# A transformer block kernel: order of the modulation groups' loads, and half of the first norm's shift as a bias

## The chip, the core and the metric
The program runs on one core of one Trainium2 chip. The metric is the device time of one execution in microseconds (us); lower is better. TensorE (PE) multiplies, VectorE (DVE), ScalarE (ACT) and GpSimd (POOL) work on elements, SyncE (SP) issues the loads. PSUM has eight banks of 128 x 512 float32; matmul outputs land there.

## What is computed
One layer over 256 latent and 256 context tokens of width 2048, all in float32. What matters here is its beginning:

```
mods  = silu(c) @ w_mod + b_mod            # 2048 x 12288, for c and for c_ctx
n     = rmsnorm(h) * gain * (1 + scale) + shift      # the first norm: amul = gain * (1 + scale)
proj  = n @ w_in                           # columns: 512 q, 256 kv, 64 rotary, then 3 x 1024 for a short convolution
q_a   = rmsnorm(q), kv_a = rmsnorm(kv), the rotary part is rotated
```

Context tokens need the kv and rotary columns alone. Attention, the convolution's gating, an output projection, routing to 4 of 32 experts and the experts' products follow.

## The kernel before, in words
The rows of the model's width lie on the 128 partitions: 16 row blocks k, four of them a set s. nT holds the transposed, normed tokens, columns 0 to 255 latent, 256 to 511 context. w_mod is worked in groups of 512 columns. Group g = s holds the shift of set s, group g = 4 + s its scale. For the first eight groups in load order (n = 0 to 7) TensorE makes the row products: 16 blocks k, each a pair of instructions, four blocks at once in four column quarters of the array (`first_rows` L706, `group_rows` L695, all in bank 7). ScalarE copies the 128 x 512 result to `part` (`rows_out` L1254), TensorE transposes it back into bank 7 (`mod_cols_of` L663), VectorE reduces it into modT (`cols_out` L1565). Only then may the next group use bank 7 (`step_group` L775 waits for modT_done). Before, `MOD_ORDER` (L345) is shift 0, scale 0, shift 1, scale 1 and so on; when both of a set are there, VectorE adds the biases, forms amul, and scales and shifts the set's four latent blocks of nT (L1618 to L1633); ScalarE does so for the context (L1271 to L1278).

The input products of a set are `query_set` (16 matmuls of 256 columns, L750), `kv_set` (4 of 512 columns, twice, L767) and `rotary_set` (4 of 512 columns on half of the array's columns, L760), which accumulate over the four sets in banks 0 to 6. TensorE's order is written out by hand (L780 to L811): the products of set s stand between the rows of the groups of set s+1. Set 3 comes last, then the squares' sums (`ones` matmuls into banks 7 and 4), with the rotary matmuls (L804, L805) in between. Then come four turns of the convolution's columns (L823 to L834), each of six blocks of 16 matmuls of 256 columns (`conv_blocks` L814).

From group 8 on the row products are VectorE's: 16 steps over 128 x 512 for each group (`accumulate` L1572), two groups a turn, begun in turn 0 only after VectorE has finished the norms of q and kv (L1646 to L1665). TensorE sums them over the partitions with `mod_sum_cols` (L677), which waits for the 16 steps: group 8 between the second and the third pair of blocks of turn 0 (L830), group 9 after the third (L834).

SyncE issues all loads on one queue, in the order of its program: x, constants, ctx, group 0, group 1, the input columns of set 0 (`load_in(0)`), then groups 2 and 3 and `load_in(1)`, and so on (L393 to L438). Groups 2 to 7 use seven buffers in turn (`load_early` L407), each load waiting until TensorE used the buffer. `load_conv` (L441) and `load_group` (L420) follow; group 9's four loads wait for VectorE's steps of group 8 (`freed_by_dve` L430), and turn 1's first convolution load is issued behind them (L451 to L453).

Of the kernel before, what the change touches and what calls it, by code (L numbers as in the profile page):

```python
# [9 lines left out]
ACT = mybir.ActivationFunctionType  # L10
# [5 lines left out]
P = 128  # L16
# [94 lines left out]
def block_kernel(nc, x, c, ctx_in, c_ctx, w_mod, b_mod, attn_norm, w_in, q_a_norm, w_q_b, kv_a_norm, w_kv_b,  # L111
                 conv_w, o_norm_mla, o_norm_conv, w_out, ffn_norm, w_router, router_bias,
                 w_exp_gate, w_exp_up, w_exp_down, w_sh_gate, w_sh_up, w_sh_down, final_norm, consts, out):
    with ExitStack() as stack:
# [71 lines left out]
        WI_SEM = (2, 0, 1, 5)  # L186
# [4 lines left out]
        EARLY_USES = [4, 4, 4, 3, 3, 4, 4] + [0] * 5  # L191
        rowq, rowkv = kq[:, 0:T], kq[:, T:3 * T]
# [45 lines left out]
        def yparts_of(t):  # L238
# [13 lines left out]

        BANKS_C, BANKS_H, BANKS_B = (1, 0), (2, 3), (4, 0)
# [18 lines left out]
        ctxs_ready = sem("ctxs_ready")  # L272
        xT_lat, xT_ctx = sem("xT_lat"), sem("xT_ctx")
# [6 lines left out]
        stat_q, stat_kv, q_ready, kv_ready = (sem("stat_q"), sem("stat_kv"),  # L280
                                                        sem("q_ready"), sem("kv_ready"))
# [14 lines left out]
        rt_rows, rt_copied, rt_full, rt_sig, mask_ready, rank_full, rank_ready = (  # L296
            sem("rt_rows"), sem("rt_copied"), sem("rt_full"), sem("rt_sig"), sem("mask_ready"), sem("rank_full"),
# [7 lines left out]
        sort_in, tbl_full, tbl_out, sort_full, cols_in = (sem("sort_in"), sem("tbl_full"), sem("tbl_out"),  # L305
                                                          sem("sort_full"), sem("cols_in"))
# [62 lines left out]
        def _(sp):  # L369
# [63 lines left out]
            for s in range(1, 4):  # L433
                for n in (2 * s, 2 * s + 1):
                    load_early(n)
                if s == 1:
                    sp.wait_ge(mod_rows, 1)
                load_in(s)  # L438
# [8 lines left out]
            sp.wait_ge(q_full, 1)  # L447
# [164 lines left out]
        def _(pool):  # L612
            nc.gpsimd.memset(csT[:, :, :], 0.0).then_inc(zeroed, 1)
            nc.gpsimd.memset(upad[:, :, :], 0.0).then_inc(zeroed, 1)

# [36 lines left out]
        def _(pe):  # L652
# [67 lines left out]
            def rows_T(rows, done, side):  # L720

                for j in range(KC // 2):
                    if j >= 3:
                        pe.wait_ge(done, j - 2)
                    for k in (2 * j, 2 * j + 1):
                        for t in range(2):
                            at = T * (k % 2) + 128 * t
                            ins = nc.tensor.transpose(ps[:, 2 * (j % 3) + side, at:at + 128], rows[:, t, 128 * k:128 * k + 128],
                                                      ident)
                    ins.then_inc(xT_full, 1)  # L730

            pe.wait_ge(xs_ready, 2)
            rows_T(xs, xT_lat, 0)
            pe.wait_ge(small_done, 1)
            for k in range(8):
                first_rows(0, k)
            pe.wait_ge(ctxs_ready, 2)
            rows_T(ctxs, xT_ctx, 1)
            for k in range(8, KC):
                first_rows(0, k)  # L740
            mod_cols_of(FIRST, 0, 7)
            pe.wait_ge(modT_done, 1)
            for k in range(KC):
# [35 lines left out]

            for s in range(SETS - 1):  # L780
                query_set(s, range(4) if s == 0 else (0, 1))
                if s == 0:
                    kv_set(s, 0)
                step_group(2 * s + 2)
                if s:
                    kv_set(s, 0)
                mod_cols_of(2 * s + 2, 0, 7)
                rotary_set(s)
                if s:
                    query_set(s, (2, 3))  # L790
                step_group(2 * s + 3)
                mod_cols_of(2 * s + 3, 1, 7)
                kv_set(s, 1)
            query_set(SETS - 1, range(4))
            kv_set(SETS - 1, 0)
            rotary_set(SETS - 1)
            pe.wait_ge(modT_done, 8)
            pe.wait_ge(q_sq, 4)
            for m in range(4):
                ins = mm(ps[:, 7, 0:T], ones, squ[:, T * m:T * m + T], m == 0, m == 3)  # L800
            ins.then_inc(stat_q, 1)
            pe.wait_ge(q_out, 4)
            pe.wait_ge(kr_sum, 1)
            mm(ps[:, 2, :], cst[:, C_DUP:C_DUP + P], krs[:, :], True, True)  # L804
            mm(ps[:, 3, 0:T], cst[:, C_ROTK:C_ROTK + P], krs[:, 0:T], True, True).then_inc(kr_mm, 1)  # L805
            kv_set(SETS - 1, 1)
            pe.wait_ge(kv_out, 1)
            pe.wait_ge(kv_sq, 2)
            for m in range(2):
                ins = mm(ps[:, 4, :], ones, squ[:, 1024 + 512 * m:1536 + 512 * m], m == 0, m == 1)  # L810
            ins.then_inc(stat_kv, 1)  # L811


# [9 lines left out]
            with pe.Fori(0, 4) as i:  # L823
# [11 lines left out]
            pe.wait_ge(y_out, 8)  # L835

# [162 lines left out]
            ins.then_inc(rt_rows, 1)  # L999
# [42 lines left out]
            nc.tensor.transpose(ps[:, 6, 0:128], vrow[:, :], ident).then_inc(tbl_full, 1)  # L1042
            shared_up(0, 1, range(8, 10))
            pe.wait_ge(tbl_out, 1)
# [190 lines left out]
        def _(sc):  # L1235
# [27 lines left out]

            for j in range(KC // 2):
                sc.wait_ge(xT_full, KC // 2 + j + 1)
                copy(nT[:, 2 * j:2 * j + 2, T:2 * T], ps[:, 2 * (j % 3) + 1, :].rearrange("p (k t) -> p k t", k=2))\
                    .then_inc(xT_ctx, 1)
            rows_out(0, 7, 0, True)
            rows_out(1, 7, 1, True)
            sc.wait_ge(xT_ctx, KC // 2)  # L1270
            for s in range(SETS):  # L1271
                if s:
                    rows_out(2 * s, 7, 0, False)
                    rows_out(2 * s + 1, 7, 1, False)
                sc.wait_ge(amul_ready, s + 1)
                for k in range(4 * s, 4 * s + 4):
                    nc.scalar.activation(nT[:, k, T:2 * T], nT[:, k, T:2 * T], ACT.Identity, bias=modT[:, k, 1:2],
                                         scale=amul[:, k, 1:2]).then_inc(nT_ctx, 1)  # L1278


            for m in range(4):
                sc.wait_ge(q_full, m + 1)
                nc.scalar.activation(squ[:, T * m:T * m + T], ps[:, m, 0:T], ACT.Square).then_inc(q_sq, 1)
            sc.wait_ge(kr_full, 1)
            copy(krs[:, :], ps[:, 6, :]).then_inc(kr_sum, 1)

            def kv_square(m):
                sc.wait_ge(kv_full, m + 1)
                nc.scalar.activation(squ[:, 1024 + 512 * m:1536 + 512 * m], ps[:, 4 + m, :], ACT.Square).then_inc(kv_sq, 1)
# [118 lines left out]
            sc.wait_ge(rt_rows, 1)  # L1408
            copy(part[:, 0, 0:T], ps[:, 4, 0:T]).then_inc(rt_copied, 1)
            sc.wait_ge(rt_full, 1)  # L1410
# [110 lines left out]
        def _(ve):  # L1521
# [35 lines left out]
            ve.wait_ge(zeroed, 2)  # L1557
# [50 lines left out]
            for j in range(KC // 2):  # L1608
                ve.wait_ge(xT_full, j + 1)
                V.tensor_copy(nT[:, 2 * j:2 * j + 2, 0:T], ps[:, 2 * (j % 3), :].rearrange("p (k t) -> p k t", k=2))\  # L1610
# [4 lines left out]
            cols_out(0, MOD_ORDER[0], 7)  # L1615
            cols_out(1, MOD_ORDER[1], 7)
            ve.wait_ge(xT_lat, KC // 2)
            for s in range(SETS):  # L1618
                if s:
                    for n in (2 * s, 2 * s + 1):  # L1620
                        cols_out(n, MOD_ORDER[n], 7)
                ve.wait_ge(modT_done, 2 * s + 2)
                for at in (4 * s, 4 * (s + 4)):
                    ins = V.tensor_tensor(modT[:, at:at + 4, :], modT[:, at:at + 4, :],
                                          bT[:, at:at + 4].unsqueeze(2).to_broadcast([P, 4, 2]), ALU.add)
                link(ins)
                V.scalar_tensor_tensor(out=amul[:, 4 * s:4 * s + 4, :], in0=modT[:, 16 + 4 * s:20 + 4 * s, :], scalar=1.0,
                                       in1=vecT[:, V_AN + 4 * s:V_AN + 4 * s + 4].unsqueeze(2).to_broadcast([P, 4, 2]),
                                       op0=ALU.add, op1=ALU.mult).then_inc(amul_ready, 1)
                ve.wait_ge(amul_ready, s + 1)  # L1630
                for k in range(4 * s, 4 * s + 4):
                    V.tensor_scalar(nT[:, k, 0:T], nT[:, k, 0:T], amul[:, k, 0:1], modT[:, k, 0:1], ALU.mult, ALU.add)\
                        .then_inc(nT_lat, 1)  # L1633


            for m in range(4):
                ve.wait_ge(q_sq, m + 1)
                V.tensor_scalar(qaT[:, m, :], ps[:, m, 0:T], vecT[:, V_QN + m:V_QN + m + 1], None, ALU.mult)\
                    .then_inc(q_out, 1)

            def kv_gain(m):
                ve.wait_ge(kv_sq, m + 1)
                V.tensor_scalar(kvT[:, m, :], ps[:, 4 + m, :], vecT[:, V_KN + m:V_KN + m + 1], None, ALU.mult)\
                    .then_inc(kv_out, 1)

            kv_gain(0)  # L1646
            ve.wait_ge(stat_q, 1)
# [491 lines left out]
```

## Time and profile before

| | us |
|---|---|
| median of 3 runs (1107.96 to 1110.99) | 1109.44 |
| span of the profiled execution, first to last instruction | 1107.5 |
| TensorE busy | 1011.4 (91%) |
| VectorE busy | 549.5 (50%) |
| ScalarE busy | 221.2 (20%) |
| loaded, mean rate | 380.3 MB, 343 GB/s |

The profiled execution has no time of its own in the list of runs; its span lies 1.9 us below their median, which holds the same work and what lies around it. A timeline row is: start, duration, engine, line, operation, output<-inputs, count, and in brackets the engine's idle time before it with what ended it. Every float32 matmul is two instructions, so x32 stands for 16 matmuls. Durations of neighbours overlap a little; distances of starts tell what a piece costs. L654 is the helper that all matmuls share.

### The profile page before, as it was taken

To read this page: it belongs to the slowest core of one execution; us is meant where nothing else is said; L and a number is where in the kernel's file an instruction comes from. 1 tells how busy PE (TensorE), PEld (TensorE's weight loads), DVE (VectorE), ACT (ScalarE), POOL (GpSimd) and SP (SyncE) were. 2 spreads that over 40 slices of the span, in tenths; PEclk is the share of its full clock that TensorE was granted. 3 is DMA by queue.
4 is the path that set the end of the run, shared out by engine and by line. 5 is a ranking of instruction groups with operands and counts; after the bars stand their busy time and mean duration, and the time that the engine had idled before them with its cause. 6 is when DMAs were issued, how large, how long until landed. Compare 5 with 4: busy or idle time off the path is not lost.

```text
span 1107.5 us, 15664 instructions
## 1 busy us (share of the span) xinstructions
PE 1011.4 (91%) x6004; PEld 566.6 (51%) x6005; DVE 549.5 (50%) x1082; ACT 221.2 (20%) x442; POOL 20.3 (2%) x28
## 2 busy tenths in 40 slices
PE   3889999999999889999998999998899898998985
PEld 2534578888885345444485645433334333344421
DVE  3000186854824694985582234545246344545524
ACT  5211110000002363010341213222113112213212
POOL 0000000000002001000000000000000000000002
PEclk9899999999999999999999999999999998999998
DMA  9999979999854747999739999999999999999994
GB/s 358 389 389 389 377 232 359 372 345 328 284 181 169 256 144 262 387 387 335 230 130 367 371 405 403 406 408 407 409 409 406 408 407 408 409 407 408 409 406 180
DMA packets 158359, 380.30 MB, mean 343 GB/s; under 512 B 10498, under 2 KB 44112, under 8 KB 157136
## 3 DMA queue, kind: packets, MB, share of 16 engines
q1 hardware_dynamic: 158288, 379.35, 91.3%
q8 instruction: 45, 0.74, 0.3%
q14 instruction: 26, 0.21, 0.1%
HBM read 377.22 MB, written 2.10 MB: 342 GB/s over the span
## 4 chain that ended last, share of the span: by engine, by line
PE 64%; DMA 13%; SPq 12%; DVE 6%; issue 2%; ACT 2%; POOL 0%; ACTq 0%; DVEq 0%; POOLq 0%
PE ps L654 64%; DMA ring<-in_w_exp_down 7%; SPq L537 4%; SPq L532 4%; DVE part L1590 3%; DMA ring<-in_w_exp_up 2%; DMA ring<-in_w_in 1%; DMA ring<-in_w_mod 1%; DMA qnT<-in_w_mod 1%; SPq L397 1%; DVE tiny L1736 1%; SPq L417 1%; DVE xres L2021 1%; SPq L394 1%; SPq L395 0%
## 5 line engine op out<-in xcount | busy, mean ns | idle before, releaser
L654 PE MATMUL ps<-nreg,ring 128*128 128x256 f32 (+2 forms) x1312 | 306.9, 398 | 6.7 <-DVE ring L1741 4.1
L654 PEld LDWEIGHTS ps<-nreg,ring 128*128 128x128 f32 (+1 forms) x1312 | 243.8, 190 | 63.1 <-issue 30.8
L1590 DVE SCALAR_TENSOR_TENSOR part<-ring,csT,part 128x512 f32<-128x512 f32 x232 | 174.7, 753 | 8.6
L654 PE MATMUL ps<-ring,nreg 128*32 128x512 f32 (+1 forms) x1344 | 174.2, 602 | 3.6 <-DMA ring<-in_w_exp_up 3.2
L654 PE MATMUL ps<-ring,conv 128*32 128x512 f32 (+2 forms) x688 | 104.5, 663 | 23.0 <-DMA ring<-in_w_exp_down 22.1
L654 PE MATMUL ps<-ring 128*128 128x512 f32 x256 | 110.7, 592 | 0.0
L654 PEld LDWEIGHTS ps<-ring,nreg 128*32 128x32 f32 (+1 forms) x1344 | 49.1, 115 | 111.7 <-issue 111.6
L2021 DVE TENSOR_TENSOR xres<-xres,ps 128x512 f32<-128x512 f32 x96 | 61.6, 683 | 48.9 <-PE ps L654 48.9
L654 PEld LDWEIGHTS ps<-ring 128*128 128x128 f32 x256 | 48.6, 190 | 60.4 <-issue 60.0
L654 PEld LDWEIGHTS ps<-ring,conv 128*32 128x32 f32 (+2 forms) x688 | 30.2, 125 | 88.4 <-issue 83.9
L654 PE MATMUL ps<-pick,qnT 128*128 128x128 bf16 x384 | 67.8, 221 | 2.8 <-DMA ring<-in_w_exp_up 2.8
L654 PE MATMUL ps<-nreg,conv 128*128 128x512 bf16 x228 | 57.9, 379 | 11.0 <-DVE xres L2021 8.7
L654 PE MATMUL ps<-pick,kq 128*128 128x128 bf16 x384 | 67.7, 221 | 0.0
L654 PE MATMUL ps<-pick,hb 128*128 128x128 bf16 x384 | 67.6, 220 | 0.0
L1977 DVE TENSOR_SCALAR nreg<-ps,amul,modT 128x128 f32<-128x128 f32 x96 | 32.8, 404 | 45.6 <-PE ps L654 45.6
L654 PEld LDWEIGHTS ps<-pick,qnT 128*128 128x128 bf16 x384 | 37.8, 98 | 24.4 <-issue 23.1
L2005 DVE TENSOR_TENSOR nreg<-ps,qkv 128x512 f32<-128x512 f32 x44 | 30.2, 687 | 34.6 <-PE ps L654 34.4
L1568 DVE TENSOR_REDUCE modT<-ps 128x8 f32<-128x32 f32 x8 | 1.5, 192 | 88.0 <-PE ps L669 88.0
L1996 DVE SCALAR_TENSOR_TENSOR conv<-ps,tiny,conv 128x256 f32<-128x256 f32 x12 | 5.8, 484 | 74.0 <-ACT conv L1445 74.0
L654 PEld LDWEIGHTS ps<-nreg,conv 128*128 128x128 bf16 x228 | 19.9, 97 | 41.1 <-issue 24.0
L1237 ACT ACTIVATE conv<-ps 128x256 f32<-128x256 f32 x20 | 7.7, 383 | 160.2 <-PE ps L654 139.5
L1435 ACT ACTIVATE nreg<-ps,modT,amul 128x128 f32<-128x128 f32 x96 | 35.9, 457 | 14.6 <-PE ps L654 14.6
(265 smaller groups left out, 883.9 us busy)
## 6 DMA issues: line engine op xcount, KB each, us to landing
ring<-in_w_mod SPq DMA_DIRECT2D x78, 1024.0 KB, 10.9
ring<-in_w_exp_gate SPq DMA_DIRECT2D x128, 512.0 KB, 13.6
ring<-in_w_exp_up SPq DMA_DIRECT2D x128, 512.0 KB, 15.1
ring<-in_w_exp_down SPq DMA_DIRECT2D x128, 512.0 KB, 14.4
ring<-in_w_in SPq DMA_DIRECT2D x12, 2048.0 KB, 13.4
ring<-in_w_out SPq DMA_DIRECT2D x8, 2048.0 KB, 11.6
ring<-in_w_mod SPq DMA_DIRECT2D x3, 2048.0 KB, 19.7
ring<-in_w_in SPq DMA_DIRECT2D x3, 1664.0 KB, 15.7
```

What stands on the lines that cost most here:

```text
L394: sp.dma_start(k_of(s, 8), mod_block(MOD_ORDER[0], 8 * s, 8)).then_inc(w_full[s], 16)
L397: sp.dma_start(early[q + 3], mod_block(MOD_ORDER[1], 4 * q, 4)).then_inc(unit_in[q + 3], 16)
L417: sp.dma_start(early[j % 7], mod_block(MOD_ORDER[n], 4 * q, 4)).then_inc(unit_in[j % 7], 16)
L532: sp.dma_start(unit(n)[:, 1024 * g:1024 * g + 1024], src[:, bass.ds(e, 1), q, :].rearrange("p a x -> p (a x)")).then_inc(unit_in[PLACE[n]] ...
L537: sp.dma_start(unit(n)[:, 1024 * k:1024 * k + 1024], wd[:, bass.ds(e, 1), k, 1024 * h:1024 * h + 1024].rearrange("p a x -> p (a x)"))\
L654: return nc.tensor.matmul(o, l, r, start=start, stop=stop)
L1435: ins = nc.scalar.activation(xg[:, k, :], ps[:, b % 2, 128 * j:128 * j + 128], ACT.Identity, bias=modT[:, 3 * KC + k, 0:1], scale=amul2[:, ...
L1590: ins = V.scalar_tensor_tensor(out=out_, in0=w_, scalar=scale, in1=acc_, op0=ALU.mult, op1=ALU.add)
L1736: link(V.tensor_reduce(rowmax[:, b:b + 2], ps[:, SCORE_BANK[b]:SCORE_BANK[b] + 2, :], AX.X, ALU.max))
L1977: ins = V.tensor_scalar(xg[:, k, :], ps[:, b % 2, 128 * j:128 * j + 128], amul2[:, k:k + 1], modT[:, 3 * KC + k, 0:1], ALU.mult, ALU.add)
L2005: V.tensor_tensor(ylast[n] if last else ygate[:, n % 2, :], ps[:, 4 + n % 2, :], gfB[:, 512 * n:512 * n + 512], ALU.mult)\
L2021: V.tensor_tensor(xres[:, h, cols], xres[:, h, cols], ps[:, 6 + h, :], ALU.add)\
```

## The change
- `MOD_ORDER` becomes [4, 5, 6, 2, 7, 3, 0, 1]: scales of sets 0, 1, 2, shift 2, scale 3, shift 3, and last the shifts of sets 0 and 1. `load_in(s)` comes earlier in the queue, and `WI_SEM` swaps two buffers.
- For sets 0 and 1 (`LATE = 2`) nT is only scaled. The input products of these sets are made without their shift.
- When shifts 0 and 1 are there, VectorE writes them into `shift_cols`, and TensorE multiplies them with the input columns of the eight blocks (`shift_products`, 8 matmuls of 512 and 8 of 320 columns, four at once), ScalarE copies the rows, and seven small matmuls turn them into columns (`bias_columns`). They enter as a bias: in ScalarE's squares and rotary copy, in VectorE's gain products.
- The eight latent blocks get their shift added afterwards (8 more VectorE instructions of 256 columns), for the convolution's products; their first block of turn 0 is split in two (`first_conv`).
- The first turn of the convolution loop is peeled. The squares' sums of q and kv and the rotary matmuls (`in_squares`) move behind the first two blocks of turn 0. ScalarE copies q raw first and squares it later; three operations over 512 columns become two of 256 each.
- Semaphores are joined (stat_q and stat_kv, rt_rows and rt_full, tbl_full and sort_full), TensorE's wait for kr_done moves behind the loop, and GpSimd has two more memsets (128 x 256 and 128 x 14).

```diff
-        MOD_ORDER = [g for s in range(4) for g in (s, s + 4)]
+        MOD_ORDER = [4, 5, 6, 2, 7, 3, 0, 1]
+        LATE = 2
...
+            load_in(0)
             sp.dma_start(k_of(5, 8), mod_block(MOD_ORDER[1], 0, 8)).then_inc(w_full[5], 16)
             for q in (2, 3):
                 sp.dma_start(early[q + 3], mod_block(MOD_ORDER[1], 4 * q, 4)).then_inc(unit_in[q + 3], 16)
-            load_in(0)
...
+            sp.wait_ge(mod_rows, 1)
+            load_in(1)
+            load_early(2)
+            load_in(2)
+            load_early(3)
+            load_early(4)
+            load_in(3)
+            for n in (5, 6, 7):
+                load_early(n)
...
             load_group(8, 12, mslot, freed_by_pe)
-            sp.wait_ge(q_full, 1)
+            sp.wait_ge(shift_full, 2)
             load_conv(0, 1, CONV0 + 2 * CW)
...
+            for s in range(1, SETS):
+                query_set(s, range(4))
+                step_group(2 * s)
+                kv_set(s, 0)
+                mod_cols_of(2 * s, 0, 7)
+                step_group(2 * s + 1)
+                rotary_set(s)
+                mod_cols_of(2 * s + 1, 1, 7)
                 kv_set(s, 1)
...
+            def shift_products():
+                pe.wait_ge(shift_ready, LATE)
+                pe.wait_ge(q_sq, 4)
+                for bank, at, end in ((2, 0, QL), (3, QL, WI)):
+                    for k in range(4 * LATE):
+                        ins = mm(ps[32 * (k % 4):32 * (k % 4) + 32, bank, 0:end - at], shift_cols[:, k, :],
+                                 wiq[k // 4][:, k % 4, at:end], k < 4, k >= 4 * LATE - 4)
+                    ins.then_inc(shift_full, 1)
+            def bias_columns():
+                pe.wait_ge(shift_out, 2)
+                for m in range(6):
+                    mm(ps[:, 7, 384 + 2 * m:386 + 2 * m], shift_rows[:, 128 * m:128 * m + 128], sum4[:, 0:2], True, True)
+                mm(ps[0:64, 7, 396:398], shift_rows[:, KR0:WI], sum4[:, 0:2], True, True).then_inc(shift_full, 1)
...
+            first_conv(range(4 * LATE, KC))
+            shift_products()
+            first_conv(range(4 * LATE))
+            bias_columns()
+            conv_blocks(0, 0, BANKS_C, (1,))
+            in_squares()
+            conv_blocks(0, 1, BANKS_H)
+            pe.wait_ge(kv_out, 2)
+            mod_sum_cols(8, 0)
+            pe.wait_ge(gc_out, 2)
+            pe.wait_ge(mean_wide, 2)
+            conv_blocks(0, 2, BANKS_B)
+            mod_sum_cols(9, 1)
+            with pe.Fori(1, 4) as i:
...
             kv_gain(0)
-            ve.wait_ge(stat_q, 1)
+            ve.wait_ge(stat_full, 1)
+            ve.wait_ge(kr_mm, 1)
+            ve.wait_ge(q_out, 4)
             mean_square_wide(rowq, ps[:, 7, 0:T], QL)
```

## Rows read from the trace of the kernel before

**Rows 1.** Busy time by stretch; columns: PE, PEld, DVE, ACT, POOL, clock, DMA share, GB/s

```profile
80.10:105.93 25.83, 24.48 (x128) 12.02 (x129) 2.18 (x9) 3.27 (x6) 0.00 (x0) 1.00 1.05 389
105.93:121.36 15.43, 14.71 (x80) 6.96 (x81) 0.19 (x1) 1.19 (x2) 0.00 (x0) 1.00 1.05 385
```

**Rows 2.** Chain that ended last, whole span, in order of time

```profile
65.84 14.22 DMA ring<-in_w_mod
...
91.81 14.07 DMA qnT<-in_w_mod
...
144.59 226.50 PE ps L654 x1038
```

**Rows 3.** Timeline of PE, 36 to 121 us

```profile
36.10 1.92 PE L654 MATMUL ps<-ring,csT 128*32 128x512 f32 x16 [0.28 <-DVE modT L1568]
...
80.10 1.07 PE L654 MATMUL ps<-ring,csT 128*32 128x512 f32 x8 [1.64 <-DMA ring<-in_w_mod]
81.10 3.70 PE L654 MATMUL ps<-nreg,ring 128*128 128x512 f32 x8
84.64 0.60 PE L669 MATMUL ps<-cst,part 128*128 128x128 f32 x4
85.17 5.59 PE L654 MATMUL ps<-nreg,ring 128*64 128x512 f32 x24
90.68 1.06 PE L654 MATMUL ps<-qnT,csT 128*32 128x512 f32 x8
...
116.51 1.07 PE L654 MATMUL ps<-hb,csT 128*32 128x512 f32 x8
...
118.25 1.90 PE L654 MATMUL ps<-ring,csT 128*32 128x512 f32 x16
```

**Rows 4.** Timeline of PE, 137 to 175 us

```profile
137.10 1.99 PE L654 MATMUL ps<-kq,cst 128*128 128x256 f32 x8
138.93 1.45 PE L654 MATMUL ps<-krs,cst 128*128 128x512 f32 x4
140.22 3.60 PE L654 MATMUL ps<-nreg,ring 128*128 128x512 f32 x8
144.59 1.95 PE L654 MATMUL ps<-kq,cst 128*128 128x512 f32 x4 [0.78 <-ACT kq L1289]
146.39 27.79 PE L654 MATMUL ps<-nreg,ring 128*128 128x256 f32 x128
174.01 0.95 PE L654 MATMUL ps<-cst,qnT 128*128 128x1 f32 x8
```

**Rows 5.** Timeline of DVE, 140 to 166 us

```profile
140.42 0.42 DVE L1650 COPY krT<-ps 128x256 f32<-128x256 f32 x1 [0.86 <-PE ps L654]
...
142.01 1.75 DVE L1540 RECIPROCAL kq<-kq 128x256 f32<-128x256 f32 x1
144.56 0.75 DVE L1643 TENSOR_SCALAR qkv<-ps,vecT 128x512 f32<-128x512 f32 x1 [0.80 <-ACT kq L1289]
...
146.59 0.69 DVE L1535 TENSOR_SCALAR kq<-ps 128x512 f32<-128x512 f32 x1
147.97 3.35 DVE L1540 RECIPROCAL kq<-kq 128x512 f32<-128x512 f32 x1 [0.69 <-ACT kq L1296]
...
152.57 0.48 DVE L1583 TENSOR_SCALAR part<-ring,csT 128x512 f32<-128x512 f32 x1
...
164.11 1.12 DVE L1590 SCALAR_TENSOR_TENSOR qnT<-ring,csT,part 128x512 f32<-128x512 f32 x1
```

**Rows 6.** Timeline of ACT, 126 to 140 us

```profile
126.72 0.38 ACT L1283 ACTIVATE kq<-ps 128x256 f32<-128x256 f32 x1 [2.38 <-PE ps L654]
...
139.61 0.42 ACT L1296 ACTIVATE kq<-kq 128x256 f32<-128x256 f32 x1
```

**Rows 7.** Busy time by stretch, around the wait before 43.58 us; columns as in rows 1

```profile
39.90:43.50 3.60, 0.66 (x4) 0.42 (x4) 1.99 (x8) 2.01 (x5) 0.00 (x0) 1.00 1.03 389
...
44.90:48.30 3.40, 3.40 (x10) 2.69 (x9) 0.00 (x0) 0.00 (x0) 0.00 (x0) 0.53 1.05 386
```

**Rows 8.** Timeline of PE at 43.58 us

```profile
43.58 12.26 PE L654 MATMUL ps<-nreg,ring 128*128 128x256 f32 x40 [2.46 <-DMA ring<-in_w_in]
55.77 1.06 PE L654 MATMUL ps<-qkv,csT 128*32 128x512 f32 x8
```

**Rows 9.** Timeline of SP, load of turn 1's first convolution block

```profile
166.00 0.39 SPq L442 DMA_DIRECT2D ring<-in_w_in  x1
```

More of the change, by code:

```diff
@@ L718, in first_rows, with rows_T @@
                     ins.then_inc(mod_rows, 1)
-            def rows_T(rows, done, side):
-                for j in range(KC // 2):
+            def rows_T(rows, done, banks, js):
+                for j in js:
                     if j >= 3:
@@ L778, in step_group @@
                 group_rows(n, 7)
[L780 to L787, printed above, removed]
+            query_set(0, (0, 2))
+            pe.wait_ge(xT_ctx, KC // 2)
+            query_set(0, (1, 3))
+            pe.wait_ge(modT_done, 1)
+            for k in range(KC):
+                first_rows(1, k)
@@ new lines, in bias_columns, with in_squares @@
+            def bias_columns():
[3 more added lines that the diff above has]
+                mm(ps[0:64, 7, 396:398], shift_rows[:, KR0:WI], sum4[:, 0:2], True, True).then_inc(shift_full, 1)
+            def in_squares():
+                pe.wait_ge(q_sq, 8)
+                for m in range(4):
+                    ins = mm(ps[:, 7, 0:T], ones, q_squ[:, T * m:T * m + T], m == 0, m == 3)
+                ins.then_inc(stat_full, 1)
+                pe.wait_ge(kr_sum, 1)
+                mm(ps[:, 6, :], cst[:, C_DUP:C_DUP + P], krs[:, :], True, True)
+                mm(ps[:, 7, T:2 * T], cst[:, C_ROTK:C_ROTK + P], krs[:, 0:T], True, True).then_inc(kr_mm, 1)
+                pe.wait_ge(kv_out, 1)
+                pe.wait_ge(kv_sq, 2)
+                for m in range(2):
+                    ins = mm(ps[:, 4, :], ones, squ[:, 1024 + 512 * m:1536 + 512 * m], m == 0, m == 1)
+                ins.then_inc(stat_full, 1)
@@ L814, in conv_blocks, with first_conv @@
+            def first_conv(ks):
+                w = k_of(0, KC)
+                for n, k in enumerate(ks):
+                    if k < 4 * LATE:
+                        pe.wait_ge(nT_shift, k + 1)
+                    ins = mm(ps[:, BANKS_C[0], 0:T], w[:, k, 0:128], nT[:, k, 0:T], k == 4 * LATE, k == 4 * LATE - 1)
+                if ks[-1] == 4 * LATE - 1:
+                    ins.then_inc(conv_full, 1)
             def conv_blocks(i, s, banks, ms=(0, 1)):
@@ L1281, in _ @@
             for m in range(4):
                 sc.wait_ge(q_full, m + 1)
-                nc.scalar.activation(squ[:, T * m:T * m + T], ps[:, m, 0:T], ACT.Square).then_inc(q_sq, 1)
+                copy(q_raw[:, m, :], ps[:, m, 0:T]).then_inc(q_sq, 1)
+            for n in (6, 7):
+                rows_out(n, 7, n % 2, False)
+            for n in range(2):
+                sc.wait_ge(shift_full, n + 1)
+                at, end, bank = ((0, QL, 2), (QL, WI, 3))[n]
+                copy(shift_rows[:, at:end], ps[:, bank, 0:end - at]).then_inc(shift_out, 1)
@@ L1284, in _ @@
+            sc.wait_ge(shift_ready, LATE + 1)
+            for m in range(4):
+                sc.wait_ge(q_sq, m + 1)
+                nc.scalar.activation(q_squ[:, T * m:T * m + T], q_raw[:, m, :], ACT.Square, bias=in_bias[:, m, 0:1])\
+                    .then_inc(q_sq, 1)
             sc.wait_ge(kr_full, 1)
-            copy(krs[:, :], ps[:, 6, :]).then_inc(kr_sum, 1)
+            for v in range(2):
+                ins = nc.scalar.activation(krs[:, T * v:T * v + T], ps[:, 6, T * v:T * v + T], ACT.Identity,
+                                           bias=in_bias[:, 6, v:v + 1])
@@ L1287, in kv_square @@
+            ins.then_inc(kr_sum, 1)
             def kv_square(m):
                 sc.wait_ge(kv_full, m + 1)
-                nc.scalar.activation(squ[:, 1024 + 512 * m:1536 + 512 * m], ps[:, 4 + m, :], ACT.Square).then_inc(kv_sq, 1)
+                for v in range(2):
+                    ins = nc.scalar.activation(squ[:, 1024 + 512 * m + T * v:1280 + 512 * m + T * v],
+                                               ps[:, 4 + m, T * v:T * v + T], ACT.Square, bias=in_bias[:, 4 + m, v:v + 1])
+                ins.then_inc(kv_sq, 1)
@@ L1614, in _, with scale_of @@
             V.tensor_scalar(ctxs[:, 0, :], ctxs[:, 0, :], tiny[:, 10:11], None, ALU.mult).then_inc(ctxs_ready, 1)
[L1615 to L1616 removed]
             ve.wait_ge(xT_lat, KC // 2)
[L1618 to L1629 removed]
+            def scale_of(n):
+                cols_out(n, MOD_ORDER[n], 7)
+                ve.wait_ge(modT_done, n + 1)
+                at = 4 * MOD_ORDER[n]
+                link(V.tensor_tensor(modT[:, at:at + 4, :], modT[:, at:at + 4, :],
+                                     bT[:, at:at + 4].unsqueeze(2).to_broadcast([P, 4, 2]), ALU.add))
+                return V.scalar_tensor_tensor(out=amul[:, at - 16:at - 12, :], in0=modT[:, at:at + 4, :], scalar=1.0,
+                                              in1=vecT[:, V_AN + at - 16:V_AN + at - 12].unsqueeze(2).to_broadcast([P, 4, 2]),
+                                              op0=ALU.add, op1=ALU.mult)
@@ new lines, in shift_of @@
+            def shift_of(n, out_):
+                cols_out(n, MOD_ORDER[n], 7)
+                ve.wait_ge(modT_done, n + 1)
+                at = 4 * MOD_ORDER[n]
+                return V.tensor_tensor(out_, modT[:, at:at + 4, :], bT[:, at:at + 4].unsqueeze(2).to_broadcast([P, 4, 2]), ALU.add)
+            for s in range(SETS):
+                n = (0, 1, 2, 4)[s]
+                if s < LATE:
+                    scale_of(n).then_inc(amul_ready, 1)
+                else:
+                    link(scale_of(n))
+                    shift_of(n + 1, modT[:, 4 * s:4 * s + 4, :]).then_inc(amul_ready, 1)
@@ new lines, in _ @@
+                    ins.then_inc(nT_lat, 1)
+            for s in range(LATE):
+                shift_of(6 + s, shift_cols[:, 4 * s:4 * s + 4, 0:2]).then_inc(shift_ready, 1)
+                ve.wait_ge(shift_ready, s + 1)
+                ve.wait_ge(mod_rows, 2 * s + 3)
+                for k in range(4 * s, 4 * s + 4):
+                    V.tensor_scalar(nT[:, k, 0:T], nT[:, k, 0:T], shift_cols[:, k, 0:1], None, ALU.add).then_inc(nT_shift, 1)
+            ve.wait_ge(shift_full, 3)
+            V.tensor_copy(tiny[:, 16:28], ps[:, 7, 384:396])
```

139 lines of the change are left out of this document (62 added, 77 removed).

## The prediction

> **What bounds the kernel now.** I read the chain that ended last first, then busy times by stretch, then the timelines of TensorE and VectorE where the change lies. Up to 106 us the chain runs through transfers: TensorE resumes at 80.10 and at 105.93 when a group's last quarter has landed [rows 2, 3], and the core loads at 389 and 385 GB/s throughout [rows 1]. But TensorE is nearly full there too: of 25.83 us it works 24.48 [rows 1]. From 144.59 on the chain is 226.5 us of matmuls without a gap [rows 2]. So two things count: when TensorE enters the convolution turns, and whether it then still runs without a gap.
>
> The second has one neighbour that is close. VectorE starts group 8's 16 steps at 152.57, and the last ends at 164.11 + 1.12 = 165.23 [rows 5]; TensorE asks for them at 174.01 [rows 4]. That is 8.8 us of slack, and the whole change must be read against it.
>
> **Prices.** Distances of starts: a kv half set 84.64 − 81.10 = 3.54; the transposes of a group 85.17 − 84.64 = 0.53; half a query set with a rotary set 90.68 − 85.17 = 5.51; a group's rows 116.51 to 118.25 + 1.90 = 3.6 [rows 3]. 128 instructions over 256 columns take 27.6 us [rows 4], 0.216 each: 6.9 for a query set or a convolution block (32), 3.45 for 16, so the rotary set is 2.05. The q sum is 138.93 − 137.10 = 1.85, the rotary matmuls 1.3, the kv sum 146.39 − 144.59 = 1.8 [rows 4].
>
> **When the loads allow it.** Between the landings at 80.06 and 105.89 lie two groups and one set of input columns, 9856 KB: 2.68 us per 1024 KB. In the new order group 5's last quarter stands where group 6's stood, less one group (4096 KB, −10.7) and plus one set of input columns (1664 KB, +4.4): it lands at 99.5, is used by 100.5. Set by set TensorE needs 6.9 + 2 x 3.6 + 2 x 3.54 + 2.05 + 2 x 0.53 = 24.3 us, the loads 25.8, so TensorE waits there for this landing, and what happened before it (the earlier start of the products, the transposes' new place) is absorbed. Groups 6 and 7 land by 121, about when asked for. Their buffers are freed by TensorE's rows; the last of them is asked for some 7 us ahead of its use, tight, but behind others still in the queue. The first convolution load follows by 127. I cost all these moves at nothing; the cover is the queue, and without it a load of 1024 KB costs at least 2.7 us.
>
> **From 100.5 to the rotary matmuls' end.** Rotary sets 2 x 2.05 = 4.1; transposes 3 x 0.53 = 1.6; kv half sets 3 x 3.54 = 10.6; query set 3 6.9; rows of groups 6 and 7 7.2; two convolution blocks 13.8; q sum 1.85 and rotary 1.3. New: step_group stands right behind the transposes in the same bank, so it waits for VectorE's reduction, 0.4 (0.28 idle in the row of that kind [rows 3]).
>
> Shift products: 8 matmuls over 832 columns in all. A group's rows, 16 over 512 columns in the same four quarters, take 3.6 us [rows 3], so these take 3.6 x (8 x 832) / (16 x 512) = 2.9. Were the quarters to go one after another, the nearest price is 3.54 for four full matmuls: 11.5 us. I take 2.9, from the same shape.
>
> The Trainium skill, TensorE: Matmul & The Clock Gate, Measured speedup vs the span model, gives three column tiles 2.38 times the speed of one, not 3. By that ratio an estimate for four is 3.5 us and the total 0.6 later. The row of this very shape decides, and it shows nearly the full factor.
>
> Bias columns: seven matmuls with full weights and two moving columns. The row with eight instructions of one column lasts 0.95, about 0.1 each [rows 4]; 14 make 1.4, nothing at the least and 3.0 at most, at the 0.216 of an instruction with 256 columns. The same skill page, Wait — 56ns, not 53.3ns?, says that matmuls start no closer than about 25 ns apart however few columns they have; an estimate from that is 0.35, and the total 1.1 earlier. The row shows four times as much for this shape, so the sum keeps the row.
>
> Together 4.1 + 1.6 + 10.6 + 6.9 + 7.2 + 13.8 + 3.15 + 0.4 + 2.9 + 1.4 = 52.1: the rotary matmuls end at 152.6. The other work has cover: ScalarE's raw copies and squares at 0.38 each [rows 6] lie under 6.9 us of convolution block; the eight VectorE additions under the last kv half set and the convolution's first half; GpSimd's memsets under the first load.
>
> **TensorE's own finish.** in_squares now waits for kv_square(1), which stands on ScalarE behind the root of q, which waits for VectorE after the rotary matmuls: mean square 0.43, root 0.42 [rows 6], two squares 0.76 and hand-overs 0.2 make 1.8 idle. Then the kv sum 1.8 and two blocks 13.8: TensorE asks for group 8 at 170.0, 4.0 earlier than 174.01. That is all the reordering gains, after the 4.3 us of new matmuls and the two new waits (0.4 and 1.8) are paid.
>
> **VectorE's tail, the step that decides.** From 152.6, in VectorE's order: mean square 0.45 (a pass over 256 columns, as the root's 0.42 [rows 6]); rotation 142.01 − 140.42 = 1.6; reciprocal 1.75; kv gain in two halves 0.8; four q products 1.4 (inside 146.59 − 144.56 [rows 5]): it reaches kv's mean square at 158.6. Before, that stood at 146.59, so this piece is 12.0 later: the sums were moved behind two convolution blocks, and nothing of VectorE's was moved ahead of them. From there to the end of group 8's steps it was 165.23 − 146.59 = 18.6 [rows 5], with 3.35 of reciprocal in it, and no part of that is touched. So group 8 is ready at 177.3. TensorE stands idle 7.3 us, and goes on 177.3 − 174.0 = **3.3 us later** than before. Group 9 is ready at 189.9, asked for after 191: no second wait. Turn 1's first load, issued behind group 8's last step (before at 166.00 [rows 9]), is out at 178, landed by 188, needed at 193.
>
> **The clock.** After a stretch of 3.6 us with only 0.66 of work the granted clock was 0.53 of full (1.2 GHz) from 44.90 to 48.30 [rows 7]. 48 instructions then took 55.77 − 43.58 = 12.2 [rows 8] where 6.9 + 3.54 = 10.45 would do: 1.75 lost. A wait of 7.3 us is longer, so I add 1.75; bounds are 0 (the wait of 1.64 before 80.10 [rows 3] lost nothing) and twice that.
>
> **Sum.** +3.3 + 1.75 = +5.05 on a stretch after which every later stage hangs on TensorE's progress. Profile 1107.5 + 5.0 = 1112.5; the median stands 1.9 above the span, so 1109.44 + 5.05 = 1114.5.
>
> **Rivals.**
> - VectorE's tail is the wait, the clock keeps up or falls briefly: +3.3, 1112.7. For it: after the wait before 43.58 the clock fell only at 44.90, with TensorE at work again [rows 7, 8], so the fall does not follow a wait at once and here may lie inside it. Chance 0.22, on both sides of the bound.
> - TensorE stays the bound. If VectorE's way from the rotary matmuls to group 8's end took under 17.4 us, the 4.0 would stay: 1105.4, **faster**. It decides at exactly that point; the rows sum it to 24.7, and nothing in the diff starts the accumulation earlier. For it only that my reading of VectorE's order could be wrong. Chance 0.12.
> - Front and tail cancel: the chain up to 152.6 is 1.5 to 3 us shorter than my distances say, or the clock falls within the wait and is back early: +0.5 to +2.5, 1111. Chance 0.14.
> - A late load: a bubble in the queue at group 7's last quarter, or a low clock in the waits near 98, or slower shift products (towards 11.5): each delays both engines alike, +7 to +9, 1117.5. Chance 0.10.
> - The change does not do what it says: then no shift group loads last, both traces agree, 1109.4; inside the third case.
> - Forecast: 0.42.
>
> **Numbers.** The range takes the forecast, the second and fourth case and most of the third: 1109.0 to 1118.5; left out is mostly the faster case. A measurement of this kernel tells 0.3% (3.3 us) from no change. Slower by more: 0.42 + 0.11 + 0.10 = 0.63. Within: 0.11 + 0.14 = 0.25. Faster: 0.12.
>
> **What would show it.** Right: TensorE idle 6 to 8 us at about 170 before mod_sum_cols of group 8, released by VectorE; the rotary matmuls ending near 152.6; VectorE's first step of group 8 near 164.6; clock at half after it. Wrong: that wait under 2 us, or TensorE's chain reaching the end of turn 0's second pair before 168 or after 172, or the landing of group 5 off 99.5.

## The result, and the profile after

| | before | after |
|---|---|---|
| median, us | 1109.50 (4 runs, 1107.96 to 1110.99) | 1115.14 (4 runs, 1114.78 to 1116.25) |
| ratio to before, 95% interval | | 1.005 [1.0036, 1.0064] |
| span of the profiled execution | 1107.5 | 1114.4 |
| TensorE busy | 1011.4 | 1013.5 |
| VectorE busy | 549.5 | 551.6 |

The change costs 5.6 us (1115.14 − 1109.50); 1114.5 was forecast. The two totals of busy time do not tell where: the changed kernel's trace lacks 22 of TensorE's records behind 414 us (4239 where the kernel before has 4261), and work at half clock counts as busy. The chain tells.

The chain that ended last, changed kernel (start, duration, what). It answers to [rows 2]:

```profile
87.82 10.90 DMA ring<-in_w_mod
...
98.76 2.93 PE ps L666 x16
...
153.51 15.77 PE ps L666 x68
169.28 7.16 issue
176.44 83.59 PE ps L666 x390
```

Ahead of the convolution turns the last wait for a transfer is at 98.7. New is a gap of 7.16 us at 169.28, in a stretch where the chain before had none. It is booked as "issue", the name for time with no releaser that the profile can name. The timeline of TensorE around it, changed kernel, answers to [rows 3, 4]:

```profile
98.76 1.06 PE L666 MATMUL ps<-ring,csT 128*32 128x512 f32 x8 [1.30 <-DMA ring<-in_w_mod]
99.76 1.94 PE L666 MATMUL ps<-nreg,ring 128*64 128x512 f32 x8
...
120.55 1.06 PE L666 MATMUL ps<-hb,csT 128*32 128x512 f32 x8 [0.28 <-DVE modT L1637]
...
133.46 3.00 PE L666 MATMUL ps<-ring,yspare 128*32 128x512 f32 x32
136.39 3.72 PE L666 MATMUL ps<-nreg,ring 128*128 128x256 f32 x16
139.95 1.60 PE L666 MATMUL ps<-cst,hb 128*128 128x2 f32 x14
141.48 7.17 PE L666 MATMUL ps<-nreg,ring 128*128 128x256 f32 x32
148.49 1.89 PE L666 MATMUL ps<-hb,cst 128*128 128x256 f32 x8
150.22 1.45 PE L666 MATMUL ps<-krs,cst 128*128 128x512 f32 x4
153.51 1.96 PE L666 MATMUL ps<-kq,cst 128*128 128x512 f32 x4 [1.84 <-ACT kq L1356]
155.31 13.98 PE L666 MATMUL ps<-nreg,ring 128*128 128x256 f32 x64
176.44 1.84 PE L666 MATMUL ps<-cst,qnT 128*128 128x1 f32 x8 [7.16 <-issue]
178.14 15.75 PE L666 MATMUL ps<-nreg,ring 128*128 128x256 f32 x64
193.73 0.95 PE L666 MATMUL ps<-cst,qnT 128*128 128x1 f32 x8
194.54 27.87 PE L666 MATMUL ps<-nreg,ring 128*128 128x256 f32 x128
```

The row at 176.44 is group 8's sum. TensorE was ready for it at 169.28, 4.7 us earlier than before (174.01), and got it 2.4 us later. The releaser is found on VectorE, timeline of the changed kernel, answering to [rows 5]:

```profile
151.77 0.42 DVE L1604 TENSOR_SCALAR kq<-ps 128x256 f32<-128x256 f32 x1 [5.74 <-issue]
...
157.72 0.69 DVE L1604 TENSOR_SCALAR kq<-ps 128x512 f32<-128x512 f32 x1
159.10 3.35 DVE L1609 RECIPROCAL kq<-kq 128x512 f32<-128x512 f32 x1 [0.70 <-ACT kq L1365]
...
163.70 0.48 DVE L1652 TENSOR_SCALAR part<-ring,csT 128x512 f32<-128x512 f32 x1
...
175.24 1.09 DVE L1659 SCALAR_TENSOR_TENSOR qnT<-ring,csT,part 128x512 f32<-128x512 f32 x1
...
192.54 0.16 DVE L1666 COPY modT<-ps 128x4 f32 x1 [0.27 <-DVE conv L1783]
```

Group 8's last step ends at 175.24 + 1.09 = 176.33, and TensorE starts 0.1 us later. VectorE works from 151.77 on with one break, 0.70 us for ScalarE's root at 159.10, but it sat idle for 5.74 us before that. Its first step of group 8 went from 152.57 to 163.70.

Busy time by stretch, changed kernel (columns as in rows 1; the one behind POOL is the granted clock):

```profile
171.80:176.40 4.60, 0.00 (x0) 0.00 (x0) 4.42 (x7) 0.00 (x0) 0.00 (x0) 0.50 0.99 347
176.44:181.90 5.46, 5.46 (x18) 4.77 (x19) 5.21 (x8) 0.00 (x0) 0.00 (x0) 0.53 0.96 328
182.00:185.40 3.40, 3.40 (x18) 2.99 (x17) 3.22 (x6) 0.00 (x0) 0.00 (x0) 1.00 1.10 348
```

The clock fell some 2 us into the wait (0.92 granted from 169.30 to 171.70, 0.50 behind that), and TensorE came back at half clock (1.2 GHz) and kept it for about 5.1 us: from 181.50 on the granted clock is 0.99. From 176.44 to 193.73 it took 17.29 us for what took 188.72 − 174.01 = 14.71 before, so 2.6 us were lost. Turn 1 starts 5.01 us later than before (194.54 against 189.53).

Nothing is won back or lost up to the first scores, and then the profiled execution loses once more. Timeline of TensorE, kernel before:

```profile
371.96 1.95 PE L654 MATMUL ps<-ring,qnT 128*128 128x512 f32 x4 [0.88 <-DVE ring L1723]
...
394.60 1.96 PE L654 MATMUL ps<-nreg,ring 128*128 128x256 f32 x8 [2.17 <-DVE ring L1741]
```

and changed kernel:

```profile
376.97 1.96 PE L666 MATMUL ps<-ring,qnT 128*128 128x512 f32 x4 [0.88 <-DVE ring L1820]
...
399.61 3.35 PE L666 MATMUL ps<-nreg,ring 128*128 128x256 f32 x8 [2.18 <-DVE ring L1838]
```

Both stretches lie 5.01 us apart, with the same wait of 2.2 us before the second row; but the same eight instructions took 3.35 instead of 1.96 us. The granted clock from 400.5 to 403.9 was 0.57 in this execution. With the matmuls behind them that is 1.7 us more (from the second row to TensorE's next wait for VectorE 14.36 instead of 12.66), and with the 5.01 it makes up all but 0.2 of the 6.9 us between the two spans. The other three executions of the changed kernel had spans of 1113.0 to 1113.4, so part of it is this execution's own.

### The profile page after: what moved, and what is told of

The parts are those of the page before. It is cut to its first block, busy times and chain, and to the rows that moved or that the text cites. A ratio compares the mean times of both kernels' runs of the same rounds, so it can differ in the third digit from the quotient of the medians.

```text
span 1114.4 us, 15752 instructions
## 1 busy us (share of the span) xinstructions
PE 1013.5 (91%) x6028; PEld 569.5 (51%) x6051; DVE 551.6 (50%) x1094; ACT 223.3 (20%) x451; POOL 20.6 (2%) x30
## 4 chain that ended last, share of the span: by engine, by line
PE 60%; SPq 15%; DMA 13%; DVE 6%; issue 4%; ACT 2%; POOL 0%; ACTq 0%; DVEq 0%; POOLq 0%
PE ps L666 59%; SPq L542 8%; DMA ring<-in_w_exp_down 7%; SPq L547 6%; DMA ring<-in_w_mod 3%; DVE part L1659 3%; DMA ring<-in_w_exp_up 2%; DMA qkv<-in_w_mod 1%; DVE tiny L1833 1%; SPq L553 1%; DVE xres L2118 1%; PE ps L740 0%; ACT nreg L1472 0%; DVE nreg L1609 0%; ACT ring L1465 0%
## 5 line engine op out<-in xcount | busy, mean ns | idle before, releaser
L666 PE MATMUL ps<-ring,conv 128*32 128x512 f32 (+2 forms) x688 | 102.1, 647 | 25.4 <-DMA ring<-in_w_exp_down 24.6
L666 PE MATMUL ps<-nreg,conv 128*128 128x512 bf16 x207 | 53.3, 379 | 13.3 <-DVE xres L2118 8.7
## 6 DMA issues: line engine op xcount, KB each, us to landing
ring<-in_w_mod SPq DMA_DIRECT2D x78, 1024.0 KB, 11.2
```

The source lines that it names most:

```text
L666: return nc.tensor.matmul(o, l, r, start=start, stop=stop)
```

## The experiments

All nine are measured against the kernel before, run on the same chip (three series; its medians there were 1110.01, 1109.33 and 1109.29). Two numbers are read from each: the total, and when TensorE starts turn 1's blocks. The second comes from one profiled execution. Totals of two runs whose intervals overlap are not told apart.

| run | ratio to before, 95% interval | wait before group 8's sum | turn 1 starts, us |
|---|---|---|---|
| kernel before | | 0 | 189.53 |
| the change | 1.0050 [1.0036, 1.0064] | 7.16 | 194.54 |
| half of group 8 early | 0.9993 [0.9981, 1.0005] | 0 | 187.82 |
| all of group 8 early | 0.9957 [0.9944, 0.9970] | 0 | 185.08 |
| wait filled | 1.0039 [1.0025, 1.0054] | 0.30 | 193.98 |
| sums moved, nothing else | 1.0105 [1.0090, 1.0120] | 8.12 | 200.63 |
| sums ahead of the second block | 1.0013 [1.0001, 1.0024] | 0.26 | 188.99 |
| all early, kv square first | 0.9949 [0.9932, 0.9965] | 0 | 182.77 |
| kv square first, alone | 1.0062 [1.0047, 1.0077] | 9.23 | 195.53 |
| group 8 asked for later | 1.0075 [1.0059, 1.0092] | moved, 8.95 | 194.79 |
| before, quarter of group 8 early | 1.0001 [0.9989, 1.0012] | 0 | 189.53 |

### Half of group 8's steps early

```diff
             kv_gain(0)
+            accumulate(8, 0, quarters=range(2), by_feature=True)
             ve.wait_ge(stat_full, 1)
...
-            with ve.Fori(0, 4) as i:
+            def turn(i, group8):
...
+            turn(0, range(2, 4))
+            with ve.Fori(1, 4) as i:
+                turn(i, range(4))
```

> Changed kernel, but VectorE does 8 of group 8's 16 steps (about 5.8 us) in its idle time between the first kv gain and the wait for the q sum. Theory (VectorE's tail before group 8 is what TensorE waits for, and the wait costs the clock too): the wait of 7.16 us before group 8's sum falls to 1 to 2 us, no low clock follows it, the third pair of convolution blocks of turn 0 starts near 171.5 instead of 178.1, and the time is about 7.5 us under the changed kernel's, near 1107.5. Rival (the 4.3 us of added matmuls and late loads are what costs, the wait is only where TensorE gets ahead of them): the time stays within 2 us of 1115, and another wait appears later, for a load or for group 9.

Median 1108.88 us beside 1110.01 for the kernel before. Timeline of TensorE in this run:

```profile
153.96 3.04 PE L666 MATMUL ps<-kq,cst 128*128 128x512 f32 x4 [1.98 <-ACT kq L1356]
...
171.26 0.95 PE L666 MATMUL ps<-cst,qnT 128*128 128x1 f32 x8
...
186.93 1.02 PE L666 MATMUL ps<-cst,qnT 128*128 128x1 f32 x8 [0.81 <-DVE modT L1666]
```

The wait before group 8's sum is gone, and with it the loss, although every added matmul is still there: 5.6 us hung on VectorE being late. The forecast of 1107.5 was 1.4 too low. Two details were not expected. The clock fell at 154.9 here, after the wait for the kv square (0.53 up to 158.3), so TensorE was 1.7 us slower up to 171.26 and met a group 8 that was just ready. And group 9's sum now waits 0.81 us for modT: the sum of group 9 may use its bank only after VectorE took group 8's out of it, and that copy stands behind group 9's 16 steps and the convolution's taps. I had checked only the 16 steps.

### All of group 8's steps early

```diff
+            accumulate(8, 0, by_feature=True)
             ve.wait_ge(shift_full, 3)
             V.tensor_copy(tiny[:, 16:28], ps[:, 7, 384:396])
...
+            turn(0, ())
+            with ve.Fori(1, 4) as i:
+                turn(i, range(4))
```

> Changed kernel, but all 16 steps of group 8 stand in VectorE's idle time of 13.3 us before it waits for the bias columns. Theory: no wait before group 8's sum at all; TensorE starts the third pair near 170.1, 4.7 us ahead of the kernel before, if the loads of group 8 (issued from 123.4 on) land by 140; time near 1105, some 4.5 us under the kernel before. Should the fourth quarter land late, the bias copy is late by as much and the squares' sums of q take it over beyond 2.4 us. Rival (added matmuls and loads): no better than the kernel before.

Median 1104.88 us, 5.1 under the 1110.01 of the kernel before. The timeline of VectorE shows the 16 steps in the idle time that the change opened, with the loads nearly in time:

```profile
129.30 0.49 DVE L1652 TENSOR_SCALAR part<-ring,csT 128x512 f32<-128x512 f32 x1 [0.61 <-DMA ring<-in_w_mod]
129.82 11.19 DVE L1659 SCALAR_TENSOR_TENSOR part<-ring,csT,part 128x512 f32<-128x512 f32 x14
...
142.03 0.17 DVE L1728 COPY tiny<-ps 128x12 f32<-128x12 f32 x1
```

The bias copy is at 142.03 instead of 141.59, inside its cover. TensorE's timeline has no wait before the third pair:

```profile
170.38 14.06 PE L666 MATMUL ps<-nreg,ring 128*128 128x256 f32 x64
```

It starts where 170.1 was expected, and 4.4 us ahead of the kernel before. So the change as a whole does gain something on TensorE, added matmuls paid; as made it gives that away to VectorE's order. How much of the gain is the loads' order alone, no run separates; the run with the move alone, below, shows that the move brings only 0.6 us of it (TensorE asks for group 8 at 181.51 − 8.12 = 173.39 instead of 174.01).

### The wait filled with matmuls

```diff
+            pe.wait_ge(kr_done, 1)
+            for _ in range(8):
+                mm(ps[:, 6, :], ident, cst[:, 0:512], True, True)
             pe.wait_ge(kv_out, 2)
             mod_sum_cols(8, 0)
```

> Changed kernel with 8 float32 matmuls over 512 columns into a free bank (6.9 us at full clock) put into TensorE's wait before group 8's sum. They compute nothing that is used. Theory: TensorE still goes on when group 8 is ready, at 176.4, but at full clock: the sum's 8 instructions take 0.95 instead of 1.84 us and the 64 behind them 13.9 instead of 15.6; time 2.6 us under the changed kernel's, near 1112.5. If the low clock came from something else, the time stays at 1115; if the matmuls ran past the wait, it would rise.

Median 1114.12 beside 1110.01, 4.1 more, where the change alone had 5.6 and 2.6 less was expected. The intervals of the two ratios overlap, so a gain is not shown. Timeline of TensorE:

```profile
169.25 7.03 PE L666 MATMUL ps<-cst 128*128 128x512 f32 x16
176.58 1.02 PE L666 MATMUL ps<-cst,qnT 128*128 128x1 f32 x8 [0.30 <-issue]
177.47 14.06 PE L666 MATMUL ps<-nreg,ring 128*128 128x256 f32 x64
192.97 1.14 PE L666 MATMUL ps<-cst,qnT 128*128 128x1 f32 x8 [1.45 <-DVE modT L1669]
193.98 29.43 PE L666 MATMUL ps<-nreg,ring 128*128 128x256 f32 x128
...
377.97 1.95 PE L666 MATMUL ps<-ring,qnT 128*128 128x512 f32 x4 [0.88 <-DVE ring L1823]
```

The clock part is shown for its stretch: at full clock the same 64 instructions take 13.9 instead of 15.6 us. But TensorE then only arrives earlier at the next thing that VectorE owes it, waits 1.45 us, and the clock falls there (0.50 from 193.8 to 197.0; the 128 instructions take 29.43 instead of 27.87). In the changed kernel that second wait is missing because the low clock had used it up: VectorE's copy is at 192.54, TensorE asks at 193.73. So of the clock's 2.6 us hardly any was to be had: turn 1 starts only 0.56 us earlier than in the changed kernel (193.98 against 194.54), and the fall behind it takes that back, with the first scores at 377.97 against 376.97. My expectation had left out the second wait.

### The move alone, on the kernel before

```diff
-            kv_set(SETS - 1, 0)
-            rotary_set(SETS - 1)
-            pe.wait_ge(modT_done, 8)
-            pe.wait_ge(q_sq, 4)
...
+            kv_set(SETS - 1, 0)
+            rotary_set(SETS - 1)
+            kv_set(SETS - 1, 1)
+            pe.wait_ge(modT_done, 8)
+            pe.wait_ge(q_out, 4)
...
+            conv_blocks(0, 0, BANKS_C)
+            in_squares()
+            pe.wait_ge(kr_done, 1)
+            conv_blocks(0, 1, BANKS_H)
```

> Kernel before, with one thing of the change: the squares' sums of q and kv and the rotary matmuls stand behind the first two convolution blocks of turn 0 instead of ahead of them. Order of loads and shift stay as they were. Theory: VectorE reaches group 8 some 16 us later (mean square of q at 156.4, q and kv done and 16 steps at 181.7), TensorE asks at 173.7 and waits 8 us, then runs 2 us at low clock: +9.5 us, near 1119. Rival (the loss comes from the new order of loads or from the added matmuls): within 2 us of the kernel before.

The q sum, the rotary matmuls and the kv sum are unchanged and stand in in_squares. Median 1121.22 beside 1110.01: +11.2 us, where +9.5 was expected. Timeline of TensorE:

```profile
181.51 1.83 PE L654 MATMUL ps<-cst,qnT 128*128 128x1 f32 x8 [8.12 <-issue]
183.20 16.78 PE L654 MATMUL ps<-nreg,ring 128*128 128x256 f32 x64
```

This shows it most plainly: with the old loads, the old shift and no added matmul, the position of three small pieces of TensorE's work makes a wait of 8.12 us (8 expected, group 8 at 181.5 against 181.7) and costs twice what the whole change costs. Here the 64 instructions took 16.78 instead of 14.06 us, so the clock took 3.6 us in all, more than I had allowed.

### The sums ahead of the second block

```diff
             bias_columns()
-            conv_blocks(0, 0, BANKS_C, (1,))
             in_squares()
+            conv_blocks(0, 0, BANKS_C, (1,))
```

> Changed kernel with the squares' sums and the rotary matmuls right behind the bias columns, ahead of the second convolution block. Theory (VectorE's turn 0 is one serial stretch that begins at the rotary matmuls' end): TensorE waits 2 us for ScalarE's squares, the rotary matmuls end near 146.9, 4.9 earlier, group 8 is ready near 171.5 instead of 176.4, and group 9's sum, which needs modT written behind group 9's steps, can go at 187.8: TensorE waits there for about 1.5 us, a wait that the low clock hid in the changed kernel. Turn 1 starts near 188.6, 1 us ahead of the kernel before: time near 1108.5. Rival (the order of the sums does not matter): stays at 1115.

Median 1111.06 beside 1109.33. Timeline of TensorE:

```profile
143.65 1.99 PE L666 MATMUL ps<-hb,cst 128*128 128x256 f32 x8 [2.06 <-ACT hb L1345]
...
171.72 1.02 PE L666 MATMUL ps<-cst,qnT 128*128 128x1 f32 x8 [0.26 <-issue]
...
188.11 1.02 PE L666 MATMUL ps<-cst,qnT 128*128 128x1 f32 x8 [1.45 <-DVE modT L1666]
188.99 29.56 PE L666 MATMUL ps<-nreg,ring 128*128 128x256 f32 x128
```

The waits stand where they were expected: 2.06 us (2), 1.45 (1.5), and 0.26 for a group 8 that was expected at 171.5. Moving one block gives back 4 of the 5.6 us, although TensorE takes on a wait of 2.06 us for it. The total is 2.5 us above what I wrote, because the clock fell behind the wait at 188 (29.56 instead of 27.87) and I had counted none. With the two runs above, this shows VectorE's turn 0 as one serial stretch, bound to the moment at which the rotary matmuls end.

### All early, and the kv square ahead of the root

```diff
             kv_square(0)
-            square_root(rowq)
             kv_square(1)
+            square_root(rowq)
             square_root(rowkv)
```

> The kernel with all 16 steps of group 8 done early, and in it kv_square(1) moved ahead of the root of q on ScalarE, so that TensorE need not wait 1.84 us for it. Theory: with VectorE off the path TensorE is the bound, and the 1.84 us come off in full: third pair of turn 0 near 168.5, time near 1103, 6.5 us under the kernel before. Rival: another wait (group 9's sum, now asked for at 182.4) takes them.

Median 1103.41 beside 1109.33, 5.9 less (6.5 expected). Timeline of TensorE:

```profile
182.77 27.87 PE L666 MATMUL ps<-nreg,ring 128*128 128x256 f32 x128
```

TensorE's wait for the kv square is gone, and turn 1 starts 2.3 us ahead of the run without this swap (185.08). In the totals only 0.8 us of that shows (5.9 against 5.1 less), and the two intervals overlap; this profiled execution then lost 1.7 us to a low clock at 388, which the other did not.

### The kv square alone

The same swap, on the changed kernel as it is.

> Changed kernel with kv_square(1) ahead of the root of q and nothing else. Theory: TensorE loses its wait of 1.84 us and asks for group 8 at 167.4, but VectorE's stretch begins where it did, so the wait before group 8's sum grows from 7.16 to 9.0 us and the time stays at 1115 within 1 us. Rival (TensorE's own waits and matmuls make the time): 1113.

Median 1116.31 beside 1109.33. Timeline of TensorE:

```profile
176.72 1.84 PE L666 MATMUL ps<-cst,qnT 128*128 128x1 f32 x8 [9.23 <-issue]
```

The same wait, whose removal brought turn 1 forward by 2.3 us above, gains nothing here: the wait before group 8's sum grows to 9.23 us, the low clock behind it takes 3.3 us instead of 2.6, and turn 1 starts at 195.53, 1.0 later than in the changed kernel. The total is 0.3 above what I allowed. Which engine is the bound decides what a saved wait is worth.

### Group 8 asked for later

```diff
-            mod_sum_cols(8, 0)
             pe.wait_ge(gc_out, 2)
             pe.wait_ge(mean_wide, 2)
             conv_blocks(0, 2, BANKS_B)
+            mod_sum_cols(8, 0)
             mod_sum_cols(9, 1)
```

> Changed kernel in which TensorE asks for group 8's sum only behind the third pair of convolution blocks, together with group 9's. Theory: the wait of 7.16 us moves, it does not vanish: the third pair ends at 183.1, then group 9's sum waits for modT behind VectorE's steps of group 9, which cannot be before 192.7: a wait of 8 to 9 us there, turn 1 starts near 193.8 (changed kernel 194.5) plus up to 1.7 us of low clock in it: time 1114 to 1116. Rival (only the early request of group 8 costs): turn 1 starts at 185 and the time is near 1106.

Median 1117.48 beside 1109.33. Timeline of TensorE:

```profile
183.19 0.95 PE L666 MATMUL ps<-cst,qnT 128*128 128x1 f32 x8
193.09 1.84 PE L666 MATMUL ps<-cst,qnT 128*128 128x1 f32 x8 [8.95 <-DVE modT L1666]
194.79 30.10 PE L666 MATMUL ps<-nreg,ring 128*128 128x256 f32 x128
```

The wait moved by one pair of blocks and grew by 1.8 us. Asking later does not help when the same engine owes the next thing too. The time is 1.5 us above the upper end of what I wrote; in the trace the low clock after this longer wait takes 2.2 us of the 30.10 and 0.9 of the sum.

### The same help for the kernel before

```diff
                     .then_inc(q_out, 1)
+            accumulate(8, 0, quarters=range(1), by_feature=True)
```

> Kernel before with the first 4 of group 8's steps (about 3 us) in VectorE's idle time between the q gains and the first kv gain: the same help as in the runs on the changed kernel. Theory: in the kernel before VectorE is 8.8 us ahead at group 8's sum, so the slack grows to about 11.8 us and the time does not move: within 1.5 us of the kernel before. Rival (early steps are worth something by themselves, because the later turns or the loads behind them gain): 2 to 3 us faster.

Median 1109.20 beside 1109.29. VectorE is 2.75 us earlier at group 8's end (162.48 against 165.23), and TensorE's rows start at the same times (174.01, 174.82, 188.72, 189.53). These early steps are worth nothing where there is slack, so the gains above are the repair of what the change broke, plus what it had gained on TensorE.

## Why the prediction was right, point by point

- **The landing that sets the clock of the front.** Forecast 99.5, used by 100.5; the trace has 98.72 and 99.76. Right, 0.7 to 0.8 early (the forecast named no tolerance for "off 99.5"); no run settles why. From there to the first scores no row of TensorE waits for a transfer, so the moved loads had the cover that the forecast gave them.
- **From there to the rotary matmuls' end.** Forecast 52.1 us; 151.67 − 99.76 = 51.9. Shift products 2.93 against 2.9, bias columns 1.53 against 1.4, the new wait in step_group 0.28 for 0.4. Neither of the two estimates from the Trainium skill, 3.5 and 0.35 us, came true; the rows of like shape did. The ratio of 2.38 in the Trainium skill (TensorE: Matmul & The Clock Gate, Measured speedup vs the span model) is for three column tiles, and here four kept nearly the full factor; worked out from 11.5 us it gives 3.6 and not 3.5. The 25 ns of the Trainium skill (same page, Wait — 56ns, not 53.3ns?) are a floor, which the trace keeps to without reaching it: 1.53 us for 14 instructions is 0.11 each.
- **TensorE's finish.** Wait for the kv square 1.84 (1.8), ready for group 8 at 169.3 (170.0).
- **VectorE's tail, the step that decides.** Group 8 ready at 176.4 (177.3), wait 7.16 (7.3). From the rotary matmuls' end to kv's mean square 157.72 − 151.67 = 6.05 (6.0), from there to the end of the steps 18.61 (18.6); the move came to 11.1 us (12.0), since the front was 0.9 early. In the run with the move alone the first piece took 162.79 − 157.38 = 5.4, so the changed order of VectorE's own waits and its halved gain passes hold at most 0.6 of the lateness. Shown as the cause by five runs: taking it away ends the loss, making it by the move alone brings a larger one, moving the request or TensorE's own wait does not help.
- **Later than before at that point.** 2.43 us, forecast 3.3. The front's 0.9 went in here (0.7 at the landing, 0.2 behind it).
- **The clock.** Mis-sized: 1.75 was forecast, from one fall of 3.4 us; after 7.2 us of standing it cost 2.6, since the low clock lasted about 5.1 us into the work. (The row behind the price counts 40 instructions and not 48; 6.9 + 3.54 is the price of 40, so the 1.75 stands.) That the two errors, 0.9 down and 0.8 up, cancel is luck: turn 1 starts 5.01 us late where the sum said 5.05. The median of 1115.14 is 0.6 above the forecast.
- **Group 9: "no second wait".** True in the changed kernel, but not for the reason given. The step was checked against the end of the 16 steps (189.9) and not against the copy of group 8's sum behind them (192.54), 1.2 us ahead of the request. Four experiments ran into that wait (0.81, 1.45, 1.45 and 8.95 us). It also bounds the rival in which the clock keeps up: going by the run with the wait filled, turn 1 would still start 4 us or more late, an estimate from its 193.98 and the 189.53 before, and not 3.3.
- **The faster rival** (TensorE stays the bound, 4.0 us gained) did not happen, but its price was near: with VectorE's tail moved away turn 1 starts 4.45 us earlier and the kernel is 5.1 us faster than before.

The low clock at 400 us in the profiled execution was not forecast, and no run here settles what brings it: the same wait of 2.2 us stands there in all eleven traces, and the stretch behind it was 1.7 us longer in five of them.

## What to carry to other kernels

When a piece of work is moved later on the engine that is the bound, look at who else starts from its result, and how long that engine's serial work is up to the next thing it owes; here 8.8 us of slack on VectorE were not enough for a move of 11. Engines that a reordering leaves idle (13 us of VectorE here) are where the following work should be moved in the same change. And a wait that is taken away counts only as far as the next debt of the same engine; look for it before summing.

## What the runs showed of the hardware that was not expected

- After a wait of 7.16 us TensorE ran at half clock for about 5.1 us more, 2.6 us lost; after one of 8.12 us it lost 3.6 us, after 8.95 us 3.1, after 9.23 us 3.3 (178.42 − 176.72 − 0.81, and 16.3 instead of 13.9 for the 64 instructions behind): the loss did not grow in step with the wait.
- Short waits can cost about their own length once more. A wait of 1.45 us was followed by a fall of the clock in two runs (1.6 to 1.7 us lost each), and one of 1.98 us before 153.96 likewise (1.7 us lost), while one of 1.30 us (before 98.76) and one of 1.84 us (before 153.51 in the changed kernel) were not. What makes the difference is not shown.
- Filling a wait with matmuls kept the clock at full (14.06 us for the 64 instructions behind it), but the fall came at the next wait instead (granted clock 0.50 from 193.8 to 197.0), and by the first scores nothing of the 2.6 us was won.
